# A 256-token, two-block kernel on one core: head norm moved to ScalarE, gating and a weight sum reordered, token shift recast

## The chip, the cores and the metric
One core of a Trainium2 chip runs the whole program. The metric is the device time of one execution in microseconds. Three runs of the kernel before gave 888.15, 896.0 and 893.72 us, so the median is 893.72 us.

## The reference, cut to what matters
All of it is float32, 256 tokens of width 1024. The first block mixes tokens in two branches and joins them:

```
y_m    = sigmoid(o_m) * head_layer_norm(h_m, mlstm_norm_w)     # (h - mean) * rsqrt(var + eps), per head of 128
merged = sigmoid(g_a) * (y_a @ w_branch_attn) + sigmoid(g_m) * (y_m @ w_branch_mlstm)
mix    = merged @ w_out
x      = x + gate_m * rms_norm(mix, g_post_mix)                # gate_m comes from c @ w_ada + b_ada
```

Then comes a feed-forward network. The second block projects x to p and shifts p by one token for 15 tiles of 128 features:

```
p  = p + (token_shift(p) - p) * mu                             # token_shift(p)[t] = p[t-1]
a  = sigmoid(a0 + ad @ a_up)
kf = kf * (1 + (a - 1) * k_a)
```

After it come a recurrence over four chunks, a second branch with a gelu and a spatial gate, an output projection, and another feed-forward network.

## The kernel before, in words
Every weight block (512 KB as a rule) goes the same way. SyncE issues its transfer into one of six slots of `raw`. ScalarE rounds it into `whi` (`split`, line 555), VectorE subtracts to get the low part `wlo` (`prepare`, line 412), and TensorE multiplies three times for each pair of tiles: high by high, high by low, low by high (`features_out`, lines 1952 to 1954, 256 columns each; `tokens_out`, lines 1927 to 1929, and `rows_out`, lines 1899 to 1901, 512 columns each). There are four `whi`/`wlo` slots, so the split of a block waits until TensorE is done with the block four before it. A raw slot comes free when VectorE has done its step on the block, and only then does SyncE issue the block six places later.

Pieces of the `w_ada` weights (`c0`, `c1`, ...) are woven between the weight blocks. For them VectorE multiplies and adds 128x1024 elements into `acc` (lines 429 and 433), four steps to a name. Two names make a part: `part(d)` sums `acc` over partitions on TensorE (lines 1869 and 1872 for a gate), and `collect_part(d)` takes the result. `with_piece` lays a `c` name that stands right behind a weight name in `head` between that name's blocks. `c8` and `c9` together make part 4, the gate `gate_m`.

The order on every engine is written out by hand, with semaphores between engines. `step` on VectorE makes each instruction wait for the one before it. Products go alternately to bank pairs 0/1 and 2/3, and a product can start only when its pair has been given back.

The end of the first mixing runs like this. TensorE does `ba0` (w_branch_attn, 48 matmuls), half of `ba1`, the turn of `ym` (`turn_ym`, line 2157, four transposes for each half of the tokens), the other half of `ba1`, then `bm0` and `bm1` (w_branch_mlstm), part 4, `wo0` and `wo1` (w_out), and the turn of the normed x (`turn_h`, line 1965). Meanwhile VectorE takes the statistics of the heads (lines 1309 to 1329), lets ScalarE take the root, normalises the heads in eight steps (line 1335), multiplies by the output gate (line 1337), and splits the turned `ym` (line 1345). `by_gate` (line 1356) multiplies a finished product by its sigmoid gate and gives the bank pair back: `bm0` needs the pair of `ba0`. `branch_sum` (line 1361) adds the two branches, ScalarE rounds the sum (line 733), `branch_low` (line 1367) makes the low part, and `wo0` waits for it in two halves.

In the second mixing ScalarE copies each projection from its banks into `praw` (`fill_praw`, line 820; lines 827 and 829 for `lora`). `shift` on VectorE takes two steps a tile (lines 1523 and 1524). The items come in the order lora (3 tiles), k, r, v (4 tiles each), then `pv` and `pu`, which feed the gelu. The factor `1 + (a - 1) * k_a` and its product with k take eight steps on VectorE (lines 1568 and 1569).

Of the kernel before, what the change touches and what calls it, by code (L numbers as in the profile page):

```python
# [9 lines left out]
P = 128  # L10
MT = S // P
# [4 lines left out]
HM, DM = 4, 128  # L16
# [89 lines left out]
def stream():  # L106

    head = ["c0", "c1", "c2", "c3", "o_if", "qm", "km", "vm", "g0", "qa", "kva", "g1", "c4", "g2", "c5",
            "g3", "c6", "ba0", "c7", "ba1", "c8", "bm0", "bm1", "c9", "wo0", "wo1"]
    first = [x for j in range(FT // 2) for x in ([f"ff{j}"] + ([f"c{BESIDE_FF[j]}"] if j in BESIDE_FF else []))]
    first += [x for i in range(FT // 2) for x in ([f"dA{i}"] + ([f"c{BESIDE_DOWN[i]}"] if i in BESIDE_DOWN else []))]
    middle = ["lora", "k", "r", "v", "pv", "pu", "c21", "wo2a", "wo3a", "wo2b", "wo3b"]
    second = [x for j in range(FT // 2) for x in ([f"gf{j}"] + ([f"c{18 + j}"] if j in (4, 5) else []))]
    second += [f"dB{i}" for i in range(FT // 2)]
    return head + first + middle + second  # L120
# [27 lines left out]
def build(nc, A, out):  # L148
# [5 lines left out]
    with ctx:  # L154
        sems = {}

        def sem(name):
            if name not in sems:
                sems[name] = ctx.enter_context(nc.semaphore(name))
            return sems[name]  # L160

        def sb(name, shape):
            return ctx.enter_context(nc.sbuf_tensor(name, shape, fp))
# [348 lines left out]
        def _(act):  # L512
# [14 lines left out]
            def freed(name, ins):  # L527
                ins.then_inc(sem(f"pair{place[name][0] % 2}_free"), 1)
# [193 lines left out]
            act.wait_ge(sem("hvar_ready"), 1)  # L722
            act.activation(st[:, 112:120], st[:, 112:120], ACT.Sqrt).then_inc(sem("hstd_ready"), 1)
            split("bm0", slice(1, 2))
            for m in range(MT):
# [90 lines left out]
            split("lora", slice(3, 4))  # L816

            def fill_praw(name, t0):
                for h, b in enumerate(item(name)):
                    ins = act.activation(praw[:, t0 + 2 * h:t0 + 2 * h + 2, 1:257],  # L820
                                         b[:, :].rearrange("p (t n) -> p t n", t=2), ACT.Copy)
                    ins.then_inc(sem("praw_ready"), 1) if h == 0 else freed(name, ins)
# [3 lines left out]
            b0, b1 = item("lora")  # L826
            act.activation(praw[:, 12:14, 1:257], b0[:, :].rearrange("p (t n) -> p t n", t=2), ACT.Copy)\
               .then_inc(sem("praw_ready"), 1)
            freed("lora", act.activation(praw[:, 14, 1:257], b1[:, 0:256], ACT.Copy))
            split("r", slice(0, 1))  # L830
# [13 lines left out]
            split("r", slice(3, 4))  # L844
            split("v", slice(0, 2))
            act.wait_ge(sem("heads_summed"), 1)
            act.activation(nrm[0:8, :], bank[6][0:8, 0:256], ACT.Sqrt).then_inc(sem("heads_root"), 1)
# [103 lines left out]
        def _(dve):  # L951
# [331 lines left out]
            for m in range(MT):  # L1283
# [3 lines left out]
                    .then_inc(sem("ya_ready"), 1)  # L1287
            prepare("ba1", slice(1, 3))
            gains(1, v1T[:, v1["g_pre_ffn"][0]:v1["g_pre_ffn"][1]])
# [40 lines left out]
            dve.nop().then_inc(sem("hvar_ready"), 1)  # L1330
            prepare("ba1", slice(3, 4))
            dve.wait_ge(sem("hstd_ready"), 1)
            for m in range(MT):
                for h in range(HM):
                    step(TS(intra[:, m, h, 0:128], intra[:, m, h, 0:128], mv[:, 4 * m + h, 0:1],
                            st[:, 112 + 4 * m + h:113 + 4 * m + h], ALU.subtract, ALU.mult))
                TT(ym[:, m, :].rearrange("p (h n) -> p h n", h=HM), intra[:, m, :, 0:128],
                   osig[:, m, :].rearrange("p (h n) -> p h n", h=HM), ALU.mult).then_inc(sem("ym_ready"), 1)
            prepare("ba1", slice(4, 6))
            prepare("bm0", slice(0, 1))  # L1340

            for m in range(MT):
                t = slice(m * P, (m + 1) * P)
                dve.wait_ge(sem("ymh_ready"), m + 1)
                TT(yml[:, :, t], bank[6 + m][:, :].rearrange("p (i n) -> p i n", i=4), ymh[:, :, t].bitcast(fp),
                   ALU.subtract).then_inc(sem("ym_split"), 1)
            prepare("bm0", slice(1, 2))

# [4 lines left out]
            def by_gate(name, at):  # L1353
                for h, b in enumerate(item(name)):
                    t = slice(at + 2 * h, at + 2 * h + 2)
                    step(TT(gT[:, t, :], b[:, :].rearrange("p (t n) -> p t n", t=2), gT[:, t, :], ALU.mult))
                dve.nop().then_inc(sem(f"pair{place[name][0] % 2}_free"), 1)

            def branch_sum(n):
# [9 lines left out]

            by_gate("ba0", 0)  # L1370
            by_gate("ba1", 4)
            prepare("bm1", slice(0, 4))
            by_gate("bm0", 8)
            branch_sum(0)
            prepare("bm1", slice(4, 5))
            branch_low(0)
            prepare("bm1", slice(5, 6))
            prepare("wo0", slice(0, 1))
            by_gate("bm1", 12)
            branch_sum(1)  # L1380
            prepare("wo0", slice(1, 2))
            branch_low(1)
# [16 lines left out]

            prepare("wo0", slice(2, 4))  # L1400
            prepare("wo1")
# [23 lines left out]
            prepare("ff0", slice(2, 3))  # L1425
            scale_h(1)
            prepare("ff0", slice(3, 4))

# [89 lines left out]
            def shift(t0, t1, rows_):  # L1518
                for t in range(t0, t1):
                    now = praw[0:rows_, t, 1:257]  # L1520
                    d = dtmp[0:rows_, t % 4, :]
                    mu = v2T[0:rows_, v2["mu_shift_2"][0] + t:v2["mu_shift_2"][0] + t + 1]
                    step(TT(d, praw[0:rows_, t, 0:256], now, ALU.subtract))
                    step(STT(pm[0:rows_, t, :], d, mu, now, ALU.mult, ALU.add))

# [40 lines left out]

            for j in range(4):
                step(TS(dtmp[:, j, :], av[:, j, :], 1.0, col("k_a_2", j), ALU.subtract, ALU.mult))
                step(STT(kT2[:, j, :], dtmp[:, j, :], 1.0, kT2[:, j, :], ALU.add, ALU.mult))
            prepare("v", slice(2, 3))  # L1570
# [269 lines left out]
        def _(pe):  # L1840
# [318 lines left out]

            features_out("ba1", four, (yah, yal), inside={0: turn_ym})  # L2160
            pe.wait_ge(sem("ym_split"), 2)
            features_out("bm0", four, (ymh, yml))
            features_out("bm1", four, (ymh, yml))

            part(4)
            tokens_out("wo0", 512, merged, by_halves=True)
            rows_out("wo1", merged)
# [383 lines left out]
```

## Time and profile before
| | us |
|---|---|
| runs shown (median 893.72) | 888.15, 893.72, 896.0 |
| the profiled execution | 894.63 |
| its span, first to last instruction | 892.8 |
| PE busy | 811.4 (91%) |
| PE weight loads busy | 744.1 (83%) |
| DVE busy | 651.6 (73%) |
| ACT busy | 380.7 (43%) |
| mean granted TensorE clock | 0.947 |

The profiled execution took 894.63 us, 1.83 us more than its span. Matmuls overlap, so two that start 0.12 us apart can each show 0.28 us; for TensorE the distance between starts is the measure, not the busy share. On VectorE and ScalarE, too, back-to-back instructions start a little less than one duration apart. Idle time stands in square brackets, with the instruction whose end released the engine.

### The profile page before, as it was taken

The numbers are of one execution on the slowest core, as the hardware profiler recorded it, in microseconds if no ns is written. First come the engines' busy times: TensorE is split into PE (matmuls) and PEld (weight loads), VectorE is DVE, ScalarE is ACT, GpSimd is POOL, SyncE is SP. The second block draws the span as 40 slices with busy tenths as digits, with TensorE's granted clock in tenths as the row PEclk, the third lists the DMA queues.
The fourth block names the chain that finished last, engine by engine and source line by source line (L and its number), as shares of the span: only waits on it lengthen the run. The fifth ranks groups of instructions, "written<-read, shape, count | busy, mean of one in ns | idle before, by whom it ended". The sixth has DMA issues, their size and how long they took to land.

```text
span 892.8 us, 16209 instructions
## 1 busy us (share of the span) xinstructions
PE 811.4 (91%) x6806; PEld 744.1 (83%) x6806; DVE 651.6 (73%) x868; ACT 380.7 (43%) x513; POOL 12.6 (1%) x32
## 2 busy tenths in 40 slices
PE   3599998978897999999996998989997999999995
PEld 3598997968776999999885986889966999999884
DVE  5759887747977867767876899887568768555447
ACT  3346843732246434443345673331132544444331
POOL 0100000000000000000001000000000000000000
PEclk9999998958897999999998999989998999999998
DMA  9964665742564979789883633540015569655521
GB/s 365 317 238 163 181 197 181 246 150 72 197 227 139 322 255 334 257 283 317 310 323 97 214 119 94 170 140 4 28 49 188 167 193 335 202 188 186 190 98 47
DMA packets 95829, 173.67 MB, mean 195 GB/s; under 512 B 7575, under 2 KB 55038, under 8 KB 95758
## 3 DMA queue, kind: packets, MB, share of 16 engines
q1 hardware_dynamic: 92784, 165.86, 55.6%
q0 software_dynamic: 1744, 5.84, 2.2%
q8 instruction: 53, 0.87, 0.4%
q10 hardware_dynamic: 1230, 0.95, 0.4%
q14 instruction: 18, 0.15, 0.0%
HBM read 171.58 MB, written 1.05 MB: 193 GB/s over the span
## 4 chain that ended last, share of the span: by engine, by line
PE 70%; DVE 18%; ACT 5%; issue 3%; DMA 3%; DVEq 0%; SPq 0%; ACTq 0%
PE bank L1952 11%; PE bank L1953 11%; PE bank L1954 11%; PE bank L2184 4%; PE bank L2186 4%; PE bank L2185 4%; PE bank L2354 3%; PE bank L1927 2%; PE bank L1929 2%; PE bank L1928 2%; DVE wlo L412 2%; DVE acc L433 2%; PE bank L1883 1%; DMA raw<-in_w_in 1%; ACT whi L555 1%
## 5 line engine op out<-in xcount | busy, mean ns | idle before, releaser
L555 ACT ACTIVATE whi<-raw 128x1024 fp32r<-128x1024 f32 (+2 forms) x218 | 226.9, 1050 | 295.8 <-PE bank L1954 144.6
L412 DVE TENSOR_TENSOR wlo<-raw,whi 128x1024 fp32r<-128x1024 f32 (+2 forms) x218 | 262.2, 1215 | 117.9 <-ACT whi L555 114.6
L1952 PE MATMUL bank<-hh,whi 128*128 128x256 f32 x1016 | 290.0, 285 | 4.2 <-DVE hl L1040 4.2
L1953 PE MATMUL bank<-hl,whi 128*128 128x256 f32 x1016 | 288.3, 284 | 0.0
L1954 PE MATMUL bank<-hh,wlo 128*128 128x256 f32 x1016 | 288.2, 284 | 0.0
L1952 PEld LDWEIGHTS bank<-hh,whi 128*128 128x128 f32 x1016 | 195.9, 193 | 7.0 <-issue 6.8
L1953 PEld LDWEIGHTS bank<-hl,whi 128*128 128x128 f32 x1016 | 194.9, 192 | 0.1
L1954 PEld LDWEIGHTS bank<-hh,wlo 128*128 128x128 f32 x1016 | 194.9, 192 | 0.0
L433 DVE SCALAR_TENSOR_TENSOR acc<-raw,cc,acc 128x1024 f32<-128x1024 f32 x77 | 98.6, 1281 | 7.0 <-DMA raw<-in_w_ada 3.4
L2184 PE MATMUL bank<-whi,ffh 128*128 128x512 f32 x176 | 69.6, 395 | 0.7 <-DVE wlo L412 0.7
L2185 PE MATMUL bank<-wlo,ffh 128*128 128x512 f32 x176 | 69.3, 393 | 0.0
L2186 PE MATMUL bank<-whi,ffl 128*128 128x512 f32 x176 | 69.2, 393 | 0.0
L1927 PE MATMUL bank<-whi,hh 128*128 128x512 f32 (+2 forms) x112 | 43.7, 390 | 5.7 <-DVE wlo L412 4.1
L1929 PE MATMUL bank<-whi,hl 128*128 128x512 f32 (+2 forms) x112 | 42.8, 382 | 0.0
L1928 PE MATMUL bank<-wlo,hh 128*128 128x512 f32 (+2 forms) x112 | 42.6, 380 | 0.0
L2184 PEld LDWEIGHTS bank<-whi,ffh 128*128 128x128 f32 x176 | 33.1, 188 | 9.1 <-DVE wlo L412 1.6
L2186 PEld LDWEIGHTS bank<-whi,ffl 128*128 128x128 f32 x176 | 33.1, 188 | 7.6
L2185 PEld LDWEIGHTS bank<-wlo,ffh 128*128 128x128 f32 x176 | 33.0, 188 | 7.4
L794 ACT ACTIVATE ffh<-arena 128x512 fp32r<-128x512 f32 x22 | 13.9, 632 | 46.1 <-DVEq L1445 46.1
L1927 PEld LDWEIGHTS bank<-whi,hh 128*128 128x128 f32 x112 | 23.5, 210 | 10.6 <-issue 3.9
L2354 PE MATMUL bank<-arena 64*64 64x64 f32 x896 | 29.4, 224 | 0.0
L2354 PEld LDWEIGHTS bank<-arena 64*64 64x64 f32 x896 | 28.6, 141 | 0.7 <-issue 0.7
(426 smaller groups left out, 1019.7 us busy)
## 6 DMA issues: line engine op xcount, KB each, us to landing
raw<-in_w_ada SPq DMA_DIRECT2D x96, 512.0 KB, 5.2
raw<-in_w_in SPq DMA_DIRECT2D x54, 512.0 KB, 4.5
raw<-in_w_ffn_in SPq DMA_DIRECT2D x88, 256.0 KB, 3.5
raw<-in_w_ffn_gate SPq DMA_DIRECT2D x44, 256.0 KB, 3.8
raw<-in_w_ffn_up SPq DMA_DIRECT2D x44, 256.0 KB, 5.1
raw<-in_w_ffn_down SPq DMA_DIRECT2D x22, 512.0 KB, 5.5
raw<-in_w_ffn_out SPq DMA_DIRECT2D x22, 512.0 KB, 3.2
raw<-in_w_out SPq DMA_DIRECT2D x16, 512.0 KB, 5.0
```

Source lines behind the costliest of these rows:

```text
L412: eng.tensor_tensor(wlo[:, g % HL, 0:nk * width], raw[:, b % RAW, 0:nk * width], whi[:, g % HL, 0:nk * width].bitcast(fp), ALU.subtract)\
L433: eng.scalar_tensor_tensor(to, x, by, to, ALU.mult, ALU.add)\
L555: act.activation(whi[:, g % HL, 0:nk * width], raw[:, b % RAW, 0:nk * width], ACT.Copy)\
L1927: mm(dsts[m], xh[:, kk_, t], wh[:, k, c], start=first, stop=False)
L1929: last = mm(dsts[m], xl[:, kk_, t], wh[:, k, c], start=False, stop=end)
L1952: mm(o, wh[:, k, c], xh[:, kk_, :], start=first, stop=False)
L1953: mm(o, wh[:, k, c], xl[:, kk_, :], start=False, stop=False)
L1954: last = mm(o, wl[:, k, c], xh[:, kk_, :], start=False, stop=end)
L2184: mm(o, ffh[:, t, x], wh[:, 0, cs], start=(t == 0), stop=False)
L2185: mm(o, ffh[:, t, x], wl[:, 0, cs], start=False, stop=False)
L2186: return mm(o, ffl[:, t, x], wh[:, 0, cs], start=False, stop=(t == FT - 1))
L2354: last = mm(bank[4 + 2 * (n % 2) + h][r, L * (q % 8):L * (q % 8) + L], lhsT[r, q, :], rhs[r, q, :], start=True, stop=True)
```

## The change
In the list of work `c8` and `c9` each move back by one or two names, so that `ba1` and `bm0` have no piece between their blocks, `bm1` has `c8` and `wo0` has `c9`. On TensorE the turn of `ym` comes after all of `ba1`, and `part(4)` comes after `wo0` instead of before it. ScalarE normalises the heads in eight ACTIVATEs with a scale and a bias column each; the bias (minus mean times inverse deviation) is one small VectorE step. Meanwhile VectorE does `by_gate("ba0")`.

In the second mixing ScalarE also writes `(1 - mu) * p` for each of the 15 tiles into `pm`, and VectorE adds `mu * p[t-1]` in one step. The factor `1 - k_a + k_a * a` becomes four ACTIVATEs into `kTt`, and VectorE multiplies by it in one step of 128x1024. The columns `1 - mu` and `1 - k_a` are made once, in two small steps.

```
-            "g3", "c6", "ba0", "c7", "ba1", "c8", "bm0", "bm1", "c9", "wo0", "wo1"]
+            "g3", "c6", "ba0", "c7", "ba1", "bm0", "bm1", "c8", "wo0", "c9", "wo1"]
 # ScalarE, first mixing
             act.activation(st[:, 112:120], st[:, 112:120], ACT.Sqrt).then_inc(sem("hstd_ready"), 1)
+            act.wait_ge(sem("hvar_ready"), 2)
+            for m in range(MT):
+                for h in range(HM):
+                    n = 4 * m + h
+                    ins = act.activation(intra[:, m, h, 0:128], intra[:, m, h, 0:128], ACT.Identity,
+                                         bias=st[:, 144 + n:145 + n], scale=st[:, 112 + n:113 + n])
+                ins.then_inc(sem("hstd_ready"), 1)
             split("bm0", slice(1, 2))
 # ScalarE, second mixing
+            def own_share(t, b, c0):
+                return act.activation(pm[:, t, :], b[:, c0:c0 + 256], ACT.Copy, scale=v2c[:, t:t + 1])
 ...
+                    act.activation(praw[:, t0 + 2 * h:t0 + 2 * h + 2, 1:257],
+                                   b[:, :].rearrange("p (t n) -> p t n", t=2), ACT.Copy)
+                    for n in range(2):
+                        ins = own_share(t0 + 2 * h + n, b, 256 * n)
                     ins.then_inc(sem("praw_ready"), 1) if h == 0 else freed(name, ins)
 ...
+            act.wait_ge(sem("lwa_ready"), 8)
+            for j in range(4):
+                a = v2["k_a_2"][0] + j
+                act.activation(kTt[:, j, :], av[:, j, :], ACT.Identity, bias=v2c[:, 15 + j:16 + j],
+                               scale=v2T[:, a:a + 1]).then_inc(sem("lwa_ready"), 1)
 # VectorE, first mixing
-            prepare("ba1", slice(1, 3))
+            prepare("ba1", slice(1, 2))
 ...
-            prepare("ba1", slice(3, 4))
+            prepare("bm0", slice(0, 1))
             dve.wait_ge(sem("hstd_ready"), 1)
-            for m in range(MT):
-                for h in range(HM):
-                    step(TS(intra[:, m, h, 0:128], intra[:, m, h, 0:128], mv[:, 4 * m + h, 0:1],
-                            st[:, 112 + 4 * m + h:113 + 4 * m + h], ALU.subtract, ALU.mult))
+            step(STT(st[:, 144:152], mv[:, :, 0], -1.0, st[:, 112:120], ALU.mult, ALU.mult))
+            dve.nop().then_inc(sem("hvar_ready"), 1)
 ...
+            by_gate("ba0", 0)
+            for m in range(MT):
+                dve.wait_ge(sem("hstd_ready"), 2 + m)
                 TT(ym[:, m, :]...                                   # as before
-            prepare("ba1", slice(4, 6))
-            prepare("bm0", slice(0, 1))
 ...
-            by_gate("ba0", 0)
             by_gate("ba1", 4)
-            prepare("bm1", slice(0, 4))
+            prepare("bm1", slice(0, 3))
             by_gate("bm0", 8)
             branch_sum(0)
-            prepare("bm1", slice(4, 5))
+            prepare("bm1", slice(3, 6))
             branch_low(0)
-            prepare("bm1", slice(5, 6))
             prepare("wo0", slice(0, 1))
             by_gate("bm1", 12)
             branch_sum(1)
-            prepare("wo0", slice(1, 2))
+            prepare("wo0", slice(1, 3))
             branch_low(1)
 ...
-            prepare("wo0", slice(2, 4))
+            prepare("wo0", slice(3, 8))
             prepare("wo1")
 # VectorE, second mixing
+            for at, name in ((0, "mu_shift_2"), (15, "k_a_2")):
+                a, z = v2[name]
+                step(TS(v2c[:, at:at + z - a], v2T[:, a:z], -1.0, 1.0, ALU.mult, ALU.add))
 ...
-                    step(TT(d, praw[0:rows_, t, 0:256], now, ALU.subtract))
-                    step(STT(pm[0:rows_, t, :], d, mu, now, ALU.mult, ALU.add))
+                    step(STT(pm[0:rows_, t, :], praw[0:rows_, t, 0:256], mu, pm[0:rows_, t, :], ALU.mult, ALU.add))
 ...
-            for j in range(4):
-                step(TS(dtmp[:, j, :], av[:, j, :], 1.0, col("k_a_2", j), ALU.subtract, ALU.mult))
-                step(STT(kT2[:, j, :], dtmp[:, j, :], 1.0, kT2[:, j, :], ALU.add, ALU.mult))
+            dve.wait_ge(sem("lwa_ready"), 12)
+            step(TT(kT2, kTt, kT2, ALU.mult))
 # TensorE
-            features_out("ba1", four, (yah, yal), inside={0: turn_ym})
+            features_out("ba1", four, (yah, yal))
+            turn_ym()
 ...
+            tokens_out("wo0", 512, merged, by_halves=True)
             part(4)
-            tokens_out("wo0", 512, merged, by_halves=True)
             rows_out("wo1", merged)
```

## Rows read from the trace of the kernel before
**Rows 1.** The page's chain that ended last, share of the span by engine.
```profile
PE 70%; DVE 18%; ACT 5%; issue 3%; DMA 3%; DVEq 0%; SPq 0%; ACTq 0%
```
**Rows 2.** Windows: stretch, length, busy us of each engine, granted clock, DMA share, GB/s.
```profile
220.00:225.00 5.00, 1.29 (x10) 1.09 (x11) 4.71 (x12) 0.60 (x1) 0.00 (x0) 1.00 0.34 105
225.00:232.00 7.00, 4.52 (x25) 4.35 (x25) 6.71 (x9) 2.60 (x3) 0.00 (x0) 0.74 0.74 238
...
286.00:340.00 54.00, 54.00 (x449) 53.04 (x448) 40.76 (x40) 24.32 (x27) 0.00 (x0) 1.00 0.88 300
...
559.00:566.00 7.00, 7.00 (x25) 5.55 (x25) 6.30 (x8) 2.35 (x2) 0.00 (x0) 0.76 0.70 216
```
**Rows 3.** TensorE's timeline, end of first mixing: start, duration, line, operation, idle before.
```profile
222.29 0.63 PE L2157 MATMUL bank<-cst,arena 128*128 128x128 f32 x4 [2.29 <-DVE arena L1337]
224.34 0.66 PE L2157 MATMUL bank<-cst,arena 128*128 128x128 f32 x4 [1.42 <-DVE arena L1337]
...
226.00 0.41 PE L1952 MATMUL bank<-yah,whi 128*128 128x256 f32 x1
226.21 0.41 PE L1953 MATMUL bank<-yal,whi 128*128 128x256 f32 x1
...
231.82 0.55 PE L1952 MATMUL bank<-ymh,whi 128*128 128x256 f32 x1 [2.48 <-issue]
...
245.97 1.12 PE L1869 MATMUL bank<-acc,cst 128*128 128x512 f32 x2 [1.05 <-DVE acc L433]
...
271.98 1.09 PE L1965 MATMUL bank<-cst,xn 128*128 128x128 f32 x8
```
**Rows 4.** VectorE's timeline, same stretch.
```profile
219.93 1.49 DVE L1335 TENSOR_SCALAR arena<-arena,st 128x128 f32<-128x128 f32 x4
...
233.37 1.23 DVE L412 TENSOR_TENSOR wlo<-raw,whi 128x1024 fp32r<-128x1024 f32 x1
234.51 1.28 DVE L433 SCALAR_TENSOR_TENSOR acc<-raw,cc,acc 128x1024 f32<-128x1024 f32 x1
...
239.28 1.42 DVE L1356 TENSOR_TENSOR arena<-bank,arena 128x512 f32<-128x512 f32 x2 [1.16 <-PE bank L1954]
240.84 1.23 DVE L1361 TENSOR_TENSOR arena<-arena 128x1024 f32<-128x1024 f32 x1
242.29 1.28 DVE L433 SCALAR_TENSOR_TENSOR acc<-raw,cc,acc 128x1024 f32<-128x1024 f32 x1 [0.22 <-DVE arena L1361]
243.49 1.22 DVE L1367 TENSOR_TENSOR mgl<-arena,mgh 128x1024 fp32r<-128x1024 f32 x1
```
**Rows 5.** ScalarE's timeline: ACTIVATEs with one column operand (L841) and with two (L568).
```profile
487.70 1.02 ACT L568 ACTIVATE arena<-bank,modT,gain 128x256 f32<-128x256 f32 x2 [1.31 <-PE bank L1965]
...
513.29 3.17 ACT L841 ACTIVATE arena<-bank,v2T 128x256 f32<-128x256 f32 x8
```
**Rows 6.** Groups by line on VectorE, 502 to 558 us: busy us, mean ns, idle before.
```profile
L1524 DVE SCALAR_TENSOR_TENSOR arena<-arena,v2T 128x256 f32<-128x256 f32 x15 | 7.3, 485 | 0.5
L1523 DVE TENSOR_TENSOR arena<-arena 128x256 f32<-128x256 f32 x15 | 6.4, 424 | 0.4
...
L1569 DVE SCALAR_TENSOR_TENSOR arena<-arena 128x256 f32<-128x256 f32 x4 | 1.7, 427 | 0.1
...
L1568 DVE TENSOR_SCALAR arena<-arena,v2T 128x256 f32<-128x256 f32 x4 | 1.4, 355 | 0.3
```
**Rows 7.** TensorE's timeline, second mixing.
```profile
521.56 1.90 PE L2224 MATMUL bank<-arena,cst 128*8 128x256 f32 x8 [0.59 <-DVEq L1549]
...
548.68 0.47 PE L1927 MATMUL bank<-whi,hh 128*128 128x512 f32 x1 [0.72 <-DVE wlo L412]
...
558.77 0.50 PE L1927 MATMUL bank<-whi,hh 128*128 128x512 f32 x1 [2.71 <-DVE wlo L412]
```
**Rows 8.** ScalarE's timeline, second mixing.
```profile
512.23 1.09 ACT L820 ACTIVATE arena<-bank 128x512 f32<-128x512 f32 x2 [1.35 <-PE bank L1954]
...
580.31 1.06 ACT L555 ACTIVATE whi<-raw 128x1024 fp32r<-128x1024 f32 x1 [4.60 <-DMA raw<-in_w_out]
```

More of the change, by code:

```diff
@@ L199, in build @@
         st = sb("st", [P, 256])
+        v2c = st[:, 64:83]
         posi = ctx.enter_context(nc.sbuf_tensor("posi", [P, MT], mybir.dt.int32))
@@ L816, in _ @@
             split("lora", slice(3, 4))
+            def own_share(t, b, c0):
+                return act.activation(pm[:, t, :], b[:, c0:c0 + 256], ACT.Copy, scale=v2c[:, t:t + 1])
             def fill_praw(name, t0):
                 for h, b in enumerate(item(name)):
-                    ins = act.activation(praw[:, t0 + 2 * h:t0 + 2 * h + 2, 1:257],
-                                         b[:, :].rearrange("p (t n) -> p t n", t=2), ACT.Copy)
+                    act.activation(praw[:, t0 + 2 * h:t0 + 2 * h + 2, 1:257],
+                                   b[:, :].rearrange("p (t n) -> p t n", t=2), ACT.Copy)
+                    for n in range(2):
+                        ins = own_share(t0 + 2 * h + n, b, 256 * n)
                     ins.then_inc(sem("praw_ready"), 1) if h == 0 else freed(name, ins)
@@ L826, in _ @@
             b0, b1 = item("lora")
-            act.activation(praw[:, 12:14, 1:257], b0[:, :].rearrange("p (t n) -> p t n", t=2), ACT.Copy)\
-               .then_inc(sem("praw_ready"), 1)
-            freed("lora", act.activation(praw[:, 14, 1:257], b1[:, 0:256], ACT.Copy))
+            act.activation(praw[:, 12:14, 1:257], b0[:, :].rearrange("p (t n) -> p t n", t=2), ACT.Copy)
+            own_share(12, b0, 0)
+            own_share(13, b0, 256).then_inc(sem("praw_ready"), 1)
+            act.activation(praw[:, 14, 1:257], b1[:, 0:256], ACT.Copy)
+            freed("lora", own_share(14, b1, 0))
             split("r", slice(0, 1))
@@ L1330, in _ @@
             dve.nop().then_inc(sem("hvar_ready"), 1)
-            prepare("ba1", slice(3, 4))
+            prepare("bm0", slice(0, 1))
             dve.wait_ge(sem("hstd_ready"), 1)
-            for m in range(MT):
-                for h in range(HM):
-                    step(TS(intra[:, m, h, 0:128], intra[:, m, h, 0:128], mv[:, 4 * m + h, 0:1],
-                            st[:, 112 + 4 * m + h:113 + 4 * m + h], ALU.subtract, ALU.mult))
-                TT(ym[:, m, :].rearrange("p (h n) -> p h n", h=HM), intra[:, m, :, 0:128],
-                   osig[:, m, :].rearrange("p (h n) -> p h n", h=HM), ALU.mult).then_inc(sem("ym_ready"), 1)
-            prepare("ba1", slice(4, 6))
-            prepare("bm0", slice(0, 1))
[L1342 to L1347, printed above, removed]
+            step(STT(st[:, 144:152], mv[:, :, 0], -1.0, st[:, 112:120], ALU.mult, ALU.mult))
+            dve.nop().then_inc(sem("hvar_ready"), 1)
             dve.wait_ge(sem("gT_ready"), 4)
@@ L1357, in by_gate @@
                 dve.nop().then_inc(sem(f"pair{place[name][0] % 2}_free"), 1)
+            by_gate("ba0", 0)
+            for m in range(MT):
+                dve.wait_ge(sem("hstd_ready"), 2 + m)
+                TT(ym[:, m, :].rearrange("p (h n) -> p h n", h=HM), intra[:, m, :, 0:128],
+                   osig[:, m, :].rearrange("p (h n) -> p h n", h=HM), ALU.mult).then_inc(sem("ym_ready"), 1)
+            for m in range(MT):
+                t = slice(m * P, (m + 1) * P)
+                dve.wait_ge(sem("ymh_ready"), m + 1)
+                TT(yml[:, :, t], bank[6 + m][:, :].rearrange("p (i n) -> p i n", i=4), ymh[:, :, t].bitcast(fp),
+                   ALU.subtract).then_inc(sem("ym_split"), 1)
+            prepare("bm0", slice(1, 2))
             def branch_sum(n):
@@ L1519, in shift @@
                 for t in range(t0, t1):
-                    now = praw[0:rows_, t, 1:257]
-                    d = dtmp[0:rows_, t % 4, :]
                     mu = v2T[0:rows_, v2["mu_shift_2"][0] + t:v2["mu_shift_2"][0] + t + 1]
-                    step(TT(d, praw[0:rows_, t, 0:256], now, ALU.subtract))
-                    step(STT(pm[0:rows_, t, :], d, mu, now, ALU.mult, ALU.add))
+                    step(STT(pm[0:rows_, t, :], praw[0:rows_, t, 0:256], mu, pm[0:rows_, t, :], ALU.mult, ALU.add))
             def shift_item(t0, t1, name, n):
```

## The prediction, made before the changed kernel was run
> **What bounds the kernel now.** I read the chain of waits first. TensorE carries 70% of it, VectorE 18% [rows 1], so a VectorE microsecond counts only where TensorE stands still for it. The windows then show where that is. In the feed-forward stretch 449 matmuls fill 54.00 us, one every 0.120 us, at clock 1.00 [rows 2]: a gain made ahead of it passes through it unchanged. The end of the first mixing is different: TensorE is busy 1.29 us of 5.00, then 4.52 of 7.00 [rows 2]. TensorE's timeline names the pauses: 2.29 and 1.42 us for the normalised heads, 2.48 us before `bm0`, 1.05 us before part 4 [rows 3]. After each of the first two groups matmuls start 0.21 us apart (226.00, 226.21), which is the 1.2 GHz level [rows 3]. The third pause has no engine's name. In the code `bm0` needs the bank pair that `by_gate("ba0")` gives back, and VectorE does that last of all, so I put it down to VectorE. In the second mixing the pauses are 0.59, 0.72 and 2.71 us, the last two for `wlo` [rows 7]: the block was split, but VectorE had not come to it.
>
> **The first mixing's end, step by step.** The anchor is 219.93, where VectorE starts normalising [rows 4]; `bm0`'s block now stands before it in place of a piece and costs the same within 0.1.
> - Removed from VectorE: eight steps, 2 x 1.5 us [rows 4]. Added: one step of 128x8; below the smallest row shown, taken as 0.2 us, bounds 0.1 and 0.35 (a step of 128x128 is 1.49/4 = 0.37).
> - Added to ScalarE: eight ACTIVATEs of 128x128 with two column operands. No row has that. The nearest, 128x256 with two, takes 1.02 for two, a spacing of 0.46; one operand gives (3.17-0.48)/7 = 0.38 [rows 5]. Halving the elements must take off something, so the bounds are 0.25 and 0.46. I take 0.36, nearer the two-operand row. Eight take 2.9: from 220.3 to 223.3. A pure multiply and add costs VectorE 0.37, so by these rows the engines are equal. The Trainium skill, "ScalarE: Activation LUTs", Rules for kernel authors, says to use VectorE for add and multiply, which can be up to about 3x faster there in bf16; the data here are float32, and that is a rival below.
> - `by_gate("ba0")` fills VectorE meanwhile (1.56 us with its signal [rows 4]); the two output-gate products (0.7 each) end at 224.0.
> - TensorE does all of `ba1` first: 96 matmuls from 211.2 at 0.119 end at 222.6, so the turns come at 222.6 and 224.1 and end at 224.8. ScalarE has to split `bm0`'s second block (1.0) before the first copy of the turned `ym`; both copies end at 225.4. VectorE's second low part ends at 226.2. `bm0` starts at 226.3, 5.5 us earlier than 231.82 [rows 3].
>
> Now VectorE is followed to `wo0`. Spacings are 1.14 for a `wlo`, 1.20 for a piece, 1.56 for a gate pair, 1.45 for a sum [rows 4]. From 226.2: `bm0`'s block, gate `ba1`, two `bm1` blocks, the first step of `c8` (0.66), giving 231.9. `bm0` ends on TensorE at 232.0 at full clock, 233.6 if one half-clock stretch stays. From 232.1 on VectorE has no idle: gate 233.7, sum 235.1, three pieces 238.7, low 239.9, `wo0` block 241.0. TensorE was through `bm1` at 237.7 and waits 3.3 us. **This is where the gain goes.** Further: gate 242.6, sum 244.0, `c9` 245.2, block 246.4, low 247.5, `c9` 248.7, block 249.9, `c9` 251.1, block 252.2, `c9` 253.4. TensorE does the third `wo0` block at 249.9 and the fourth until 255.5 (12 matmuls of 512 columns each, 2.8 us). Part 4, which began in a pause at 245.97 before, now stands alone on TensorE: 3.5 us, to 259.0. `wo1` takes 48 x 0.233 = 11.3 and ends at 270.3, against 271.98 [rows 3]: 1.7 us gained. One half-clock stretch at `bm0` takes 1.6 of it back, half clock on parts of `wo0` costs another 0.9. The bounds are thus -1.7 and +0.9. I take -0.3: TensorE is idle 1.4 us before `bm0` and has done eight transposes in the 3.7 us since `ba1`, and both such stretches before were followed by half clock [rows 3]. The transfers cause nothing: no block is issued later than VectorE frees its slot, and the nearest margin, `c8`'s last piece (issued at 227.4, wanted at 237.5), is 10 us. GpSimd's queue is not touched. The chain from `wo1` to the feed-forward network moves as a whole. The two steps that make `1 - mu` and `1 - k_a` (0.4 us) lie under `ff0`.
>
> **The second mixing.** Removed from VectorE: 15 steps of 0.424 + 0.034 wait = 0.46 us, 6.9 us, and eight of 0.355 and 0.427 (3.4 us with waits [rows 6]) against one of 1.26 us (as `branch_sum`'s 1.23 [rows 4]), 2.1 us: 9.0 in all. Added to ScalarE: 15 x 0.38 (128x256, one operand) and 4 x 0.46 (two operands) [rows 5], 7.5 us; bounds 0.29 (no operand effect) and 0.46 for each of the 15.
> - Item k: ScalarE starts its fill at 512.23 as before [rows 8], bound by TensorE. It takes 2 x (0.5 + 2 x 0.38) = 2.5 instead of 1.1 us, to 514.8. VectorE, 1.4 us early from `lora`, waits for it and gains nothing there. The squares are then ready at 519.9 and no longer hold TensorE at 521.56: 0.6 gained [rows 7].
> - `k_a`: its ACTIVATEs end at 524.0 behind the split of `v`'s second block, VectorE wants them at 530.1: no wait. The root behind them is ready at 525.7, wanted at 528.0.
> - r and v: VectorE comes to shift r at 536.7 (fill ends 534.1) and to shift v at 544.7 (fill ends 545.3, wait 0.6). `pv`'s first two blocks are low-parted at 544.7 instead of 549.7, its last two at 553.7 instead of 559.8.
> - TensorE starts `pv` at 547.4 without pausing: 0.7 gained. It wants the third block at 553.0 to 554.5 and it is there: 2.7 gained. Half clock after that pause (559 to 566 shows 0.76, [rows 2]) cost about 8 matmuls x 0.19 = 1.5, and goes with it.
>
> That is 0.6 + 0.7 + 2.7 + 1.5 = 5.5, and 0.2 for small waits: **5.7 us**. An earlier half-clock stretch, at 549 us, costs 1.5 too; I let it stand, and its going would make 7.2. The gelu, its norm and the spatial gate follow `pv` at fixed distance. The recurrence waits for the gelu of `pu`, which stands on ScalarE behind a block that waited 4.60 us for its transfer [rows 8]; the slot for it is freed by VectorE right behind the spatial norm, so it moves along.
>
> **Sum.** -0.3 - 5.7 = -6.0. Against the profiled execution, 894.63, that gives 888.6. Its time is 0.9 above the median of the runs shown, 893.72, so the forecast is **887.7 us**.
>
> **Rivals.**
> 1. Both leftover half-clock stretches go as well: -1.7 - 7.2 = -8.9, **884.8**. For: the pauses ahead of them shrink. Against: some pause stays at each place.
> 2. ScalarE becomes the late one in the second mixing. Its 7.5 us added are nearly the 9.0 removed; if VectorE waits for every fill as for k, 9.0 - 7.5 = 1.5 remain, **891.9** with the first part. Against: r's fill has 2.6 us to spare.
> 3. Slower than before: `wo0` is now done in pieces with waits between, and the clock stays at 1.2 GHz through it. Each of its 48 matmuls then costs 0.43 instead of 0.233. From 241.1 they run to 261.7 instead of 255.5, +6.2: that just undoes the -6.0. It decides once half clock reaches `wo1`; with eight of its matmuls (1.6) the time is **895.5**. For: waits of 3.3 and about 1 us in there. Against: VectorE's pace hides the first two blocks' slowness.
> 4. ScalarE normalises three times as slowly as VectorE did: 8 x 1.15 = 9.2 instead of 2.9 us, +6.3 on `bm0`, **894.0**. Against: rows 5. It is what the rule of the Trainium skill named above (same page, same section) would make of it if its bf16 factor held here.
> 5. The second mixing's gain is lost again at the gelu of `pu`, because the transfer ahead of it doesn't come earlier: **893.4**. Against: its slot is freed earlier.
>
> **How the numbers follow.** Chances: forecast 0.48, rival 1 0.25, rival 2 0.15, rival 3 0.04, rival 4 0.02, rival 5 0.06. The range reaches from below rival 1 by half the spread of its terms to past rival 2: 882.5 to 892.5. It leaves out rivals 3 to 5 (0.12) and the lower tail. Within 1% of 893.72, which is about what a measurement of this kernel can tell from no change, is 884.8 to 902.7. Rival 1 stands on that edge: half of it and a little of the forecast make 0.24 faster, 0.73 the same, 0.03 slower.
>
> **What would show it.** In the changed profile: `bm0` starts near 226.3; TensorE waits about 3 us for `wo0`, released by VectorE's `wlo`; part 4 runs after `wo0`; `wo1` ends within 2 us of before; the wait at 521.56 and both waits in `pv` are gone; the recurrence starts 5 to 8 us earlier. It is wrong if `wo0` starts before 238, if ACTIVATEs with a column operand are spaced over 0.5 us, or if TensorE still waits for a `wlo` in `pv`.

## The result, and the profile after

| | median us | lowest to highest | runs |
|---|---|---|---|
| before | 891.22 | 888.15 to 896.0 | 4 |
| after | 881.37 | 878.1 to 884.37 | 4 |

The ratio is 0.9874, with a 95% interval of 0.9836 to 0.9912: faster by 1.3%, and by the interval by 0.9 to 1.6%. The forecast was 887.7 with a range of 882.5 to 892.5, so the time fell below the range, and "the same within 1%" had the highest chance, 0.73. The sign was right, the size was not. Later runs of the same two kernels pull the numbers together: 20 runs of after have a mean of 883.3 (standard error 0.7), 81 runs of before 891.4 (0.3). By these the change is worth 8.1 us, or 0.9%, where the forecast had 6.0 off a starting point of 893.72: the change stands close to the 1% mark, and the median of the four runs shown lies beyond it.

The profiled execution of after took 883.83 us with a span of 882.0; before had 894.63 and 892.8. The page's chain that ended last, against [rows 1]:

```profile
PE 76%; DVE 15%; ACT 4%; DMA 3%; issue 2%; DVEq 0%; SPq 0%; ACTq 0%
```

Six points of the chain have passed to TensorE. The span is only 1.2% shorter, so most of that is the chain running over matmuls where it ran over other engines before, and not time saved. Where time was saved is best read by marks that both kernels have. I took seven on TensorE's timeline (the first matmul of `ba0`, of `bm0`, of `wo0`, the transposes behind `wo1`, the first of the feed-forward network, of `lora`, of the spatial gate `sg`) and subtracted:

| us from ... to ... | before | before again (e9) | after | after again (e4) | third (e12) |
|---|---|---|---|---|---|
| start to `ba0` | 211.2 | 207.5 | 213.3 | 207.8 | 212.6 |
| `ba0` to `bm0` | 20.6 | 20.6 | 14.9 | 14.9 | 14.9 |
| `ba0` to transposes | 60.8 | 60.8 | 59.6 | 59.6 | 59.6 |
| transposes to `lora` | 218.3 | 218.4 | 217.6 | 217.5 | 217.4 |
| `lora` to `sg` | 84.0 | 84.1 | 75.8 | 76.1 | 75.9 |
| `sg` to the end | 318.5 | 318.4 | 315.7 | 316.2 | 318.6 |

Between the profiled execution of before and the first of after lie 10.8 us: 1.2 in the first mixing, 0.7 in the feed-forward stretch, 8.2 in the second mixing, 2.8 behind the spatial gate, less 2.1 in the start, which the change does not touch. The last two items can't be put down to the change. The start moves by 3.7 us in before and by 5.5 in after. The stretch behind the spatial gate was 315.7 and 318.6 in two executions of the same kernel after; the two profiles of before have 318.5 and 318.4, which is too few to say how often it is shorter there.

Windows of after, placed as those in [rows 2] were (columns as there): the first three at the same distance behind `ba0` or the start of the feed-forward network, the last at the same distance ahead of `sg`:

```profile
222.00:227.00 5.00, 4.15 (x33) 3.52 (x31) 3.02 (x6) 4.82 (x11) 0.00 (x0) 1.00 0.38 108
227.00:234.00 7.00, 5.82 (x49) 5.82 (x50) 6.58 (x8) 2.30 (x3) 0.00 (x0) 1.00 0.38 103
287.00:341.00 54.00, 54.00 (x449) 53.04 (x448) 41.54 (x41) 23.86 (x27) 0.00 (x0) 1.00 0.88 301
551.00:558.00 7.00, 7.00 (x32) 5.68 (x32) 6.75 (x9) 3.41 (x3) 0.00 (x0) 1.00 0.56 161
```

In the first window VectorE has fallen from 4.71 us to 3.02 and ScalarE has risen from 0.60 to 4.82: the normalisation has changed engines, and TensorE is busy 4.15 us instead of 1.29. The clock of the second is 1.00 instead of 0.74. The feed-forward window is the same to a hundredth. The last, in `pv`, holds 32 matmuls where 25 stood, at 1.00 instead of 0.76.

TensorE's timeline at the end of the first mixing, for [rows 3]:

```profile
224.87 0.63 PE L2177 MATMUL bank<-cst,arena 128*128 128x128 f32 x4
226.11 0.66 PE L2177 MATMUL bank<-cst,arena 128*128 128x128 f32 x4 [0.62 <-DVE arena L1371]
228.18 0.39 PE L1972 MATMUL bank<-ymh,whi 128*128 128x256 f32 x1 [1.41 <-DVE yml L1377]
...
243.66 0.47 PE L1947 MATMUL bank<-whi,mgh 128*128 128x512 f32 x1 [3.84 <-DVE wlo L413]
...
244.25 0.63 PE L1949 MATMUL bank<-whi,mgl 128*128 128x512 f32 x1
244.68 0.63 PE L1947 MATMUL bank<-whi,mgh 128*128 128x512 f32 x1
...
248.95 0.50 PE L1947 MATMUL bank<-whi,mgh 128*128 128x512 f32 x1 [0.72 <-DVE wlo L413]
...
252.41 0.50 PE L1947 MATMUL bank<-whi,mgh 128*128 128x512 f32 x1 [0.41 <-DVE wlo L413]
...
258.08 1.02 PE L1889 MATMUL bank<-acc,cst 128*128 128x512 f32 x2
...
261.50 0.48 PE L1919 MATMUL bank<-whi,mgh 128*128 128x512 f32 x1
...
272.89 0.87 PE L1985 MATMUL bank<-cst,xn 128*128 128x128 f32 x6
```

The pauses of 2.29, 1.42 and 2.48 us are now none, 0.62 and 1.41, and one of 3.84 stands ahead of `wo0`, released by a `wlo` of VectorE. The matmuls behind it start 0.43 us apart (244.25, 244.68), the 1.2 GHz level ("half clock" below), until 247.6; part 4 fills 258.08 to 261.50 alone. ScalarE and VectorE, for [rows 4] and [rows 5]:

```profile
222.14 3.20 ACT L729 ACTIVATE arena<-arena,st 128x128 f32<-128x128 f32 x8 [1.24 <-DVEq L1355]
225.24 1.04 ACT L556 ACTIVATE whi<-raw 128x1024 fp32r<-128x1024 f32 x1
226.19 1.22 ACT L735 ACTIVATE ymh<-bank 128x512 fp32r<-128x512 f32 x2
```

```profile
221.88 0.16 DVE L1354 SCALAR_TENSOR_TENSOR st<-st 128x8 f32<-128x8 f32 x1
222.47 1.42 DVE L1364 TENSOR_TENSOR arena<-bank,arena 128x512 f32<-128x512 f32 x2 [0.42 <-PE bank L1974]
224.03 0.69 DVE L1371 TENSOR_TENSOR arena<-arena 128x512 f32<-128x512 f32 x1
225.37 0.69 DVE L1371 TENSOR_TENSOR arena<-arena 128x512 f32<-128x512 f32 x1 [0.65 <-ACT arena L729]
226.80 1.33 DVE L1377 TENSOR_TENSOR yml<-bank,ymh 128x512 fp32r<-128x512 f32 x2 [0.74 <-ACT ymh L735]
```

Eight ACTIVATEs take 222.14 to 225.24, where the next one starts: 0.39 each. `by_gate("ba0")` at 222.47 lies beside them.

In the second mixing TensorE's timeline shows no pause at all between `lora` and the spatial gate; the three of [rows 7] are gone. The new groups of VectorE, 502 to 558 us, and of ScalarE, 500 to 550 us, for [rows 6]:

```profile
L1545 DVE SCALAR_TENSOR_TENSOR arena<-arena,v2T 128x256 f32<-128x256 f32 x15 | 7.3, 485 | 2.1 <-ACT arena L827 1.7
```

```profile
L827 ACT ACTIVATE arena<-bank,st 128x256 f32<-128x256 f32 x15 | 6.4, 485 | 0.0
```

One VectorE step a tile instead of two, with waits of 2.1 us in all for ScalarE's own shares.

### The profile page after: what moved, and what is told of

It reads as the page before. It is cut to its first block, busy times and chain, and to the rows that moved or that the text cites. A ratio compares the mean times of both kernels' runs of the same rounds, so it can differ in the third digit from the quotient of the medians.

```text
span 882.0 us, 16211 instructions
## 1 busy us (share of the span) xinstructions
PE 803.9 (91%) x6806; PEld 735.9 (83%) x6806; DVE 641.8 (73%) x841; ACT 391.1 (44%) x540; POOL 12.7 (1%) x32
## 4 chain that ended last, share of the span: by engine, by line
PE 76%; DVE 15%; ACT 4%; DMA 3%; issue 2%; DVEq 0%; SPq 0%; ACTq 0%
PE bank L1972 13%; PE bank L1973 13%; PE bank L1974 13%; PE bank L2205 4%; PE bank L2207 4%; PE bank L2206 4%; PE bank L2375 3%; DVE acc L434 2%; PE bank L1947 2%; PE bank L1948 2%; PE bank L1949 2%; DVE wlo L413 2%; PE bank L1903 1%; DVE arena L434 1%; DMA raw<-in_w_ada 1%
```

## The experiments

Twelve runs followed, in three groups. "Before" below is the kernel before as it ran in the same group: 890.8 (28 runs), 894.11 (12), 890.84 (25). Stretches are those of the table above.

**The parts alone.** Three kernels made of before: e1 has only the first mixing's end, e2 only the second mixing's edits (shift and `k_a`), e3 only the shift. e4 is the whole change again.

```diff
 e3, from before:
-step(TT(d, praw[0:rows_, t, 0:256], now, ALU.subtract))
-step(STT(pm[0:rows_, t, :], d, mu, now, ALU.mult, ALU.add))
+step(STT(pm[0:rows_, t, :], praw[0:rows_, t, 0:256], mu, pm[0:rows_, t, :], ALU.mult, ALU.add))
 ... and own_share() behind each of ScalarE's fills, as in the change
```

> Only the first mixing's part (order of work, ScalarE normalising, gates, turn, part 4 behind wo0); the second mixing as before. Theory A (the terms of the prediction hold and the second mixing was mis-sized): 0.5 to 2 us faster than before, and the profile keeps the pauses of 0.7 and 2.7 us in pv and the half-clock stretch at the start of the recurrence. Rival B (the first mixing gave more than the profile of the changed kernel shows, because executions differ in their first 200 us): 4 us or more faster.

> Only the second mixing's part (own share and k_a on ScalarE, one VectorE step a tile). Theory A: 8 to 11 us faster than before: 5.7 of waits and one half-clock stretch as predicted, 1.5 for the stretch in pv that I let stand, and 0 to 3 for the half-clock stretch at the recurrence's start, which I did not count. Rival B: 5 to 6 us, as predicted, and the rest of the measured gain belongs to the first mixing or to chance.

> Only the token shift; k_a in eight VectorE steps as before. VectorE keeps 2.1 of the 9.0 us. Theory A: pv's first two blocks are ready 2.1 us later than in the whole change (544.1 instead of 542 on its clock) and TensorE wants them at 547, so nothing is lost there; the third block is ready at 555.1 instead of 553 and TensorE wants it at 553, so about 2 us and possibly one half-clock stretch (1.5) come back: 4 to 7 us faster than before. Rival (VectorE was relieved by more than needed, k_a is worth nothing): the same as the second part alone within 1 us.

> The changed kernel once more, for its scatter and for the parts' sum. Theory A: ratio 0.985 to 0.991 against before, and the parts (first alone, second alone) add up to it within 2 us; in its profile neither pv nor the recurrence's start shows half clock. Rival (chance): the ratio comes nearer to 0.993, which is my forecast's 6 us, and the half-clock stretch at the recurrence's start is there again.

| | median (runs) | ratio | `ba0` to transposes | `lora` to `sg` |
|---|---|---|---|---|
| e1 first only | 892.33 (12) | 1.0002 [0.9978, 1.0027] | 60.9 | 84.0 |
| e2 second only | 886.91 (12) | 0.9946 [0.992, 0.9971] | 60.7 | 76.4 |
| e3 shift only | 886.03 (8) | 0.9942 [0.9917, 0.9966] | 60.7 | 77.1 |
| e4 whole | 884.07 (9) | 0.9918 [0.9888, 0.9948] | 59.6 | 76.1 |

In the traces the shift is nearly everything: it takes 6.9 us out of its stretch, and `k_a` 0.7 more. In the times e2 and e3 can't be told apart. Against my expectations: e3 lies within its 4 to 7 us (4.8 by the medians); e1 misses its 0.5 to 2, e2 its 8 to 11 (3.9 by the medians, 5.0 by the means), and e4, at 0.9918, its 0.985 to 0.991. The first part alone starts `bm0` 5.7 us earlier and gains nothing in the time. In its profiled execution the matmuls at `bm0` start 0.21 us apart, as they did before:

```profile
222.21 0.58 PE L1958 MATMUL bank<-ymh,whi 128*128 128x256 f32 x1 [1.41 <-DVE yml L1363]
...
222.81 0.41 PE L1960 MATMUL bank<-ymh,wlo 128*128 128x256 f32 x1
223.02 0.41 PE L1958 MATMUL bank<-ymh,whi 128*128 128x256 f32 x1
```

The pause of 1.41 us and what stands ahead of it are those of after, where the clock stayed at 2.4 GHz.

**The four combinations again, and before as its own control.** Copies of before, e1, e2 and after in one group.

> The kernel before once more, unchanged, to see how far its own stretches move between executions. Ratio 1.00 within 0.003. Theory A (the stretches that the change touches repeat): ba0 to bm0 20.6, ba0 to the transposes behind wo1 60.8 +-0.3 and lora's start to the spatial gate's first matmul 84.0 +-0.3, while the start up to ba0 falls anywhere from 207 to 214 us and the stretch from the spatial gate to the end anywhere from 315.6 to 318.8, with or without half clock at the recurrence's start. Rival B (the recurrence's half-clock stretch belongs to this kernel and went with the change): spatial gate to end is 318.5 +-0.3 again, with 6.8 us of half clock at its start.

> The first mixing's part alone, once more, in one group with before, the shift part and the whole. Theory A: ba0 to the transposes behind wo1 59.6 to 61.0 (before 60.8), by whether half clock falls into bm0 and wo0; the median of times within 0.3% of before, ratio 0.997 to 1.001. Rival B (the parts add up and the whole's gain of 8 us holds a share from here): ratio 0.995 to 0.996.

> The token shift and the k_a part alone, once more. Theory A: lora's start to the spatial gate's first matmul 76.4 +-0.4 (before 84.0), ratio 0.990 to 0.993, the times' median 6.5 to 8.5 us below before. Rival B (what the trace shows here is partly lost later, as the first group of runs had it, 0.9946): ratio 0.994 to 0.996.

> The whole change a third time, so that all four combinations of the two parts share their runs of before. Theory A: ba0 to the transposes 59.6 +-0.2, lora to the spatial gate 75.9 +-0.3, ratio 0.989 to 0.992, which is the shift part's ratio times 0.998. Rival B (the two parts are worth more together than singly): ratio below 0.988 with the shift part alone above 0.993.

| | median (runs) | ratio | start to `ba0` | `ba0` to transposes | `lora` to `sg` |
|---|---|---|---|---|---|
| e9 before | 893.25 (12) | 1.0023 [1.0006, 1.0041] | 207.5 | 60.8 | 84.1 |
| e10 first only | 891.97 (12) | 1.0006 [0.9983, 1.0028] | 213.9 | 59.6 | 85.3 |
| e11 second only | 886.74 (7) | 0.9941 [0.9919, 0.9962] | 213.3 | 60.8 | 76.3 |
| e12 whole | 885.58 (7) | 0.9922 [0.9895, 0.995] | 212.6 | 59.6 | 75.9 |

Before against itself gives 1.0023, with 1 outside the interval: a quarter of a per cent is what such a comparison can be off by. My expectation that e11 would come to 0.990 to 0.993 failed, and its rival's 0.994 to 0.996 came: the 7.7 us in its trace show as 4.1 in the medians. e12 lies just outside its 0.989 to 0.992. The copy of before has `sg` to the end at 318.4 once more, as rival B said; but e3 has 318.8, and e12, the whole change, 318.6, so that stretch did not go with the change. The windows from 14 us behind `sg`, of the first execution of after and then of e12, show the clock at 1.00 and at 0.66:

```profile
580.00:590.00 10.00, 7.17 (x239) 6.89 (x235) 8.81 (x13) 2.39 (x4) 0.00 (x0) 1.00 0.21 73
```

```profile
579.00:589.00 10.00, 6.95 (x150) 6.82 (x148) 8.11 (x11) 1.65 (x3) 0.00 (x0) 0.66 0.34 119
```

e10 shows how half clock and a pause trade places. Its first block of `pv` starts behind nearly the same pause as before's (0.72 [rows 7]), but at full clock, where before had 0.57 (its window stands further down). TensorE is then done with that block 1.5 us sooner and waits 4.29 us instead of 2.71 for the same `wlo`; half clock follows:

```profile
550.44 0.47 PE L1933 MATMUL bank<-whi,hh 128*128 128x512 f32 x1 [0.71 <-DVE wlo L412]
```

```profile
551.00:555.00 4.00, 4.00 (x19) 3.25 (x18) 3.75 (x9) 1.06 (x1) 0.00 (x0) 1.00 0.81 259
```

```profile
560.54 0.79 PE L1933 MATMUL bank<-whi,hh 128*128 128x512 f32 x1 [4.29 <-DVE wlo L412]
```

```profile
558.00:565.00 7.00, 4.46 (x11) 3.49 (x12) 6.68 (x10) 0.00 (x0) 0.00 (x0) 0.54 0.43 142
```

The stretch from `lora` to `sg` is 1.3 us longer there than in before. Half of that has happened by the first pause behind `lora` (31.9 us behind it instead of 31.3): 25 matmuls at `lora` start 0.21 us apart, where before has 19. The rest lies behind the pause of 4.29, with 10 slow matmuls for 7. The windows over the start of `lora`, before and then e10:

```profile
490.00:498.00 8.00, 7.72 (x49) 7.75 (x50) 6.31 (x11) 4.61 (x7) 1.31 (x4) 0.71 0.85 274
```

```profile
491.00:499.00 8.00, 7.60 (x43) 7.63 (x44) 6.28 (x10) 3.79 (x7) 1.08 (x2) 0.62 0.85 255
```

Over both groups 24 runs of the first part alone have a mean of 891.4, before's own; 19 of the second alone 885.9; 20 of the whole 883.3. The whole is 2.6 us better than its parts added, with a standard error of about 1.1 on that. The traces agree. From `ba0` to `sg` before has 363.1 and 363.2 us, the first part alone 364.0 and 362.8, the second alone 355.4 and 355.8, the whole 353.0, 353.1 and 352.8: 10.1 us for the whole, some 7.4 for the parts added. What e1 and e10 lose again they lose to the clock, each in another place (e1 at `bm0` and at the start of the feed-forward network, e10 at `lora` and in `pv`). Why the whole, with the same first part, did not lose it in any of its three profiles stays open. So does this: the traces give the second part 7.6 us and the whole 10.1, the means of the times 5.5 and 8.1.

**Two costs added to after.** e5 gives VectorE back the step that the shift lost, as a dead subtraction a tile; e6 makes ScalarE write each own share twice.

```diff
 e5, from after:
+step(TT(dtmp[0:rows_, t % 4, :], praw[0:rows_, t, 0:256], praw[0:rows_, t, 1:257], ALU.subtract))
 e6, from after, in own_share():
+act.activation(to, b[:, c0:c0 + 256], ACT.Copy, scale=v2c[:, t:t + 1])        # to: room that nobody reads
```

> The whole change, plus VectorE's subtraction for each of the 15 tiles as before the change, into a buffer that nobody reads: VectorE gets back 6.9 of the 9.0 us, ScalarE keeps all its new work. Measured from the first matmul of lora to the first spatial-gate matmul (84.0 us before, 75.8 in the whole change). Theory A (the gain is VectorE time that TensorE waited for): 81 to 84 us, with pauses and half clock in pv again, and the time 5 to 8 us above the whole change. Rival C (the gain came from splitting the work onto ScalarE's copies, earlier or later semaphores): 76 to 78 us.

> The whole change, with ScalarE's own share of each of the 15 tiles computed twice (the extra one into unused room): ScalarE gets 15 x 0.38 = 5.7 us more in the second mixing, VectorE nothing. Theory A: the fills for k and v, where VectorE already waits 0.6 and 0.4 us, become 1.5 us longer; VectorE had 5 us in hand at pv, so the stretch lora to spatial gate grows by 0 to 2 us (76 to 78). Rival 2 of the prediction (ScalarE is the next to be late): 80 us or more.

e5: 885.52 (5 runs), ratio 0.9926 [0.9895, 0.9958]; `lora` to `sg` 82.0. e6: 882.9 (4 runs), 0.99 [0.9863, 0.9937]; 77.5. So 6.4 us more on VectorE lengthen the stretch by 6.1, and some 5.2 us on ScalarE (15 at a spacing of 0.35) by 1.5: VectorE paces it, ScalarE has some room. In time e5 is less clear than in its trace: 5 to 8 us above the whole were expected. Its mean of 886.3 is 3.0 above the 883.3 of after, and its ratio of 0.9926 is hardly above e4's and e12's (0.9918 and 0.9922). Their pauses ahead of a block of `pv`, and the clock behind, e5 first:

```profile
550.83 0.51 PE L1948 MATMUL bank<-whi,hh 128*128 128x512 f32 x1 [2.88 <-DVE wlo L413]
```

```profile
552.00:556.00 4.00, 4.00 (x13) 3.14 (x12) 3.75 (x6) 0.60 (x1) 0.00 (x0) 0.57 0.73 250
```

```profile
548.25 0.50 PE L1954 MATMUL bank<-whi,hh 128*128 128x512 f32 x1 [0.89 <-DVE wlo L413]
```

```profile
548.00:552.00 4.00, 3.75 (x16) 3.11 (x17) 3.75 (x7) 1.15 (x2) 0.00 (x0) 1.00 0.67 198
```

In e5 half clock (0.57) follows the pause. In e6 one of 0.89 doesn't, though before's pause of 0.72 [rows 7] was followed by this:

```profile
549.00:553.00 4.00, 4.00 (x12) 3.14 (x11) 3.75 (x9) 0.00 (x0) 0.00 (x0) 0.57 0.76 246
```

**The normalisation back on VectorE.** e7 is after, with the eight steps on VectorE behind `by_gate("ba0")`, and without ScalarE's eight ACTIVATEs and the small step for their bias.

```diff
 ... in VectorE's loop over m:
-dve.wait_ge(sem("hstd_ready"), 2 + m)
+for h in range(HM):
+    step(TS(intra[:, m, h, 0:128], intra[:, m, h, 0:128], mv[:, 4 * m + h, 0:1],
+            st[:, 112 + 4 * m + h:113 + 4 * m + h], ALU.subtract, ALU.mult))
```

> The whole change with its order, but the heads normalised by VectorE in eight steps as before the change, after the gate of ba0. Theory A (VectorE sets the pace to wo0): the eight steps (3.0) stand on VectorE's chain, minus the 0.2 of the small step and the wait for ScalarE (0.65) and for the copies; bm0 starts 1 to 2.5 us later than in the whole change (14.9 us after ba0 there), and wo1 ends 1 to 2.5 us later (59.6 after ba0). Rival (TensorE's own work and part 4 set it): bm0 later, wo1's end within 0.5 us.

It took 881.99 (4 runs), ratio 0.9884 [0.9851, 0.9916]. In the trace `bm0` starts 16.7 us behind `ba0` instead of 14.9, and the transposes come at 62.8 instead of 59.6. Two of VectorE's rows and TensorE's at `bm0`:

```profile
218.12 1.50 DVE L1362 TENSOR_SCALAR arena<-arena,st 128x128 f32<-128x128 f32 x4
...
220.27 1.49 DVE L1362 TENSOR_SCALAR arena<-arena,st 128x128 f32<-128x128 f32 x4
```

```profile
225.40 0.41 PE L1967 MATMUL bank<-ymh,wlo 128*128 128x256 f32 x1
225.61 0.41 PE L1965 MATMUL bank<-ymh,whi 128*128 128x256 f32 x1
```

1.8 us are VectorE's order, the rest is half clock at `bm0`, which this execution had and after's three did not. The transposes are 3.2 us later, past the 1 to 2.5 that I expected. That the time is no longer, I can't explain from one profile and four runs; whether the change of engine is worth anything beyond the reordering stays open.

**Part 4 moved again.** e8 puts part 4 between the two halves of `wo1` and `c9` behind it, to cover the 3.4 us.

```diff
-            "g3", "c6", "ba0", "c7", "ba1", "bm0", "bm1", "c8", "wo0", "c9", "wo1"]
+            "g3", "c6", "ba0", "c7", "ba1", "bm0", "bm1", "c8", "wo0", "wo1", "c9"]
...
-            part(4)
-            rows_out("wo1", merged)
+            rows_out("wo1", merged, between=lambda: part(4))
```

> A candidate: the whole change, with c9 moved from beside wo0 to beside wo1, and part 4 on TensorE between the two halves of wo1. Theory A (TensorE waits for VectorE at wo0, and c9's four pieces of 1.2 us stand in that chain): wo0's four blocks follow each other without waits; wo1 ends 2.5 to 4.5 us earlier than in the whole change (59.6 us after ba0 there), so 55 to 57, and the time falls 2 to 4.5 us below the whole change. Rival (transfers or the post-norm chain take over, because c9's last piece and the gate's collection now come late): 58 us or more from ba0 to the turn, or the turn earlier and the feed-forward start not.

It took 885.44 (6 runs), ratio 0.9907 [0.9879, 0.9935]; `ba0` to the transposes is 60.6, not 55 to 57. `wo1` itself is through 1.5 us earlier than in after (57.9 us behind `ba0` instead of 59.4). But there is a new wait on VectorE, and behind it one on TensorE:

```profile
263.55 1.42 DVE L1018 TENSOR_TENSOR gg<-bank,bc 128x512 f32<-128x512 f32 x2 [4.13 <-PE bank L1892]
```

```profile
271.45 0.77 PE L1987 MATMUL bank<-cst,xn 128*128 128x128 f32 x5 [2.45 <-DVE xn L1443]
```

The gate vector that part 4 makes is wanted for the first token tile as soon as its half of `wo1` is done, and VectorE stands idle 4.13 us for it. My sum had left this consumer out; the rival of the expectation had named it ("the gate's collection now come late").

## Why the prediction was wrong

Point by point, by its own steps; predicted times of the start are moved by the 2.1 us that `ba0` came later.

- **Start of `bm0`: right.** 228.4 forecast, 228.18 measured. The ACTIVATE that no row showed takes 0.39 instead of 0.36, the 128x8 step 0.16 instead of 0.2. Rival 4 (1.15 each) is out; the factor that the Trainium skill, "ScalarE: Activation LUTs", Rules for kernel authors, gives for bf16 has no counterpart in these float32 rows, where VectorE's step takes 0.37 and ScalarE's 0.39.
- **A half-clock stretch at `bm0`: wrong place.** It came at `wo0` instead, behind the pause of 3.84, in all three executions of after; eight matmuls there 0.43 us apart instead of 0.233 are 1.5 us, and most of it was hidden, since TensorE waited for VectorE's next two blocks anyway (0.72 and 0.41). e1 shows that `bm0` can have it too, with the same pause ahead.
- **`wo0`, part 4, `wo1`: right in its steps, small in its gain.** `wo0` was forecast at 243.1 and came at 243.66 with a wait of 3.84 (3.3 forecast), part 4 took 3.42 (3.5). The end came 1.2 us earlier; I had taken 0.3, between bounds of 1.7 earlier and 0.9 later, because I let half clock at `bm0` take most of it back. In the time, though, e1 and e10 make the first part worth nothing alone.
- **The second mixing: the step that failed.** The three pauses went as forecast (0.6, 0.7, 2.7), and the half-clock stretch behind the last one (1.5). "An earlier half-clock stretch, at 549 us, costs 1.5 too; I let it stand": it went. In after, e2 and e3 TensorE runs through `pv` at 1.00. That is 7.0 to 7.2, against 7.6 and 7.7 measured in e2 and e11 and 6.9 in e3, which kept a pause of 0.30. The prediction had no ground for letting it stand. Its own step says that `pv` starts "without pausing", and its word against rival 1 is that "some pause stays at each place"; both can't hold. In all ten profiles in which `pv` starts without a pause its first block ran at full clock; in the four with a pause of 0.71 to 0.73 it ran at half clock three times.
- **The start of `lora`: a term put at nothing.** The whole has 8.0 to 8.2 where the second part alone has 7.6 and 7.7. At `lora` 12 to 15 matmuls are slow in the whole, 17 and 18 in e11 and e2, and 19 in before; at 0.09 us each that is the difference. e8, with 27, has 77.3 us for the stretch.
- **The pause is not independent of the stretch.** I had priced "pause" and "half clock" as separate terms. While VectorE paced `pv`, half clock at 549 was hidden in the following wait: e10 lost that stretch and waited 4.29 instead of 2.71. Only when no pause is left does every slow matmul count, and then none was slow.
- **The feed-forward stretch passes a gain on unchanged: off by 0.7.** I read the window from 286 us and took no row of the 5 us just before it, where the network starts. There the clock changed:

```profile
276.00:287.00 11.00, 7.95 (x38) 7.58 (x39) 8.10 (x13) 6.17 (x13) 1.05 (x2) 0.53 0.45 132
```

```profile
277.00:288.00 11.00, 8.04 (x47) 7.67 (x48) 8.73 (x16) 6.71 (x13) 1.05 (x2) 0.69 0.41 130
```

  (before, then after, both from 5 us ahead of the network's first matmul): 47 matmuls instead of 38 in the same time. In the profiles without the first part 23 to 25 matmuls are slow there, in those with it 12 to 16, but in e1 27.
- **The rivals.** Rival 1, given 0.25, is what happened in kind: its 8.9 lies between the 8.1 of all runs and the 10.1 of the traces. Rival 2 had ScalarE late for every fill; VectorE waits 2.1 us for its shares in all, and e6 shows room left. Rival 3 had the right clock event at the right place and overrated it, as its own "against" said. In rival 5 the wait for `w_out`'s transfer ahead of `pu`'s gelu is there unchanged at 4.60 us, and moved along:

```profile
572.62 1.06 ACT L556 ACTIVATE whi<-raw 128x1024 fp32r<-128x1024 f32 x1 [4.60 <-DMA raw<-in_w_out]
```

- **The baseline.** 893.72 was the median of three runs; 81 have 891.4. That alone puts the forecast 2.3 too high. The rest of the miss, 4.0, is 2.1 of mechanism (8.1 against 6.0, by the means) and 1.9 by which the four runs shown lie under the mean of 20.

So of 6.3 us between 887.7 and 881.37 a third is mis-sized terms of the sum, and the others are two small samples. By the traces the mechanism was off by more, 4.1 us from `ba0` to `sg` (10.1 against 6.0): 0.9 in the first mixing, 0.7 in the feed-forward stretch, and 2.5 in the second mixing, 1.5 of it the stretch at 549 us and some 0.6 the clock at `lora`. The 2 us by which the times show less are not explained. The range was too narrow for all of this.

## What to carry to other kernels

When a change removes the last pauses of a stretch, price the half clock inside it as going too, and check it both ways: behind a remaining pause it may be hidden, without one it counts in full. A step that only starts something earlier is worth what the next pacing engine leaves of it; look for that engine's next block and for every consumer of what is moved. Hold every "against" next to the steps of the sum: here one said that a pause stays at a place where the other had taken it away. Before a forecast of absolute time, ask how far untouched stretches differ between executions, and widen the range by that.

## What the runs showed of the hardware that was not expected

The start, which the change does not touch, differs between executions. In the windows from 22 to 43 us, before and after:

```profile
22.00:43.00 21.00, 12.03 (x54) 11.04 (x54) 17.42 (x27) 8.18 (x12) 3.88 (x7) 1.00 0.95 322
```

```profile
22.00:43.00 21.00, 11.35 (x42) 10.19 (x42) 17.49 (x27) 8.18 (x12) 3.90 (x7) 0.51 0.94 321
```

The clock is 1.00 or 0.51 with the same program and transfers. Where it was 0.51 or 0.52 (after, e2, e10, e11, e12), `ba0` came at 212.6 to 213.9 us; where it was 1.00, at 207.0 to 208.0 in seven profiles and at 211.2 and 210.9 in before and e8, which lost time to the clock later in the start. So an untouched stretch moves by 6 us, nearly the size of the whole effect. The 81 times of before are spread accordingly, from 885.7 to 896.0: 29 lie below 890.1, 33 above 892.3, and 19 between. How much of that is the start is not shown for runs without a profile. What sets the clock there I did not test.

The pause right ahead does not decide alone whether half clock follows: 1.41 us was followed by full clock in after and by half clock in e1 and e7; at the same block of `pv`, 0.71 by full clock in e10 and 0.72 by half clock in before.
